# Weight sums of the third branch product issued behind those of the second, and the first gate loads moved behind them

## The reference, cut to what matters

```
o_a = hgrn2_mixer(q_a, f_a, i_a, g_a, lb_table[l], hg_norm[l])
o_b = swa_mixer(q_b, k_b, v_b, positions, sw_sinks[l])
y_a = o_a @ w_proj_a[l]          # (512 x 1024) @ (1024 x 2048)
y_b = o_b @ w_proj_b[l]
merged = sigmoid(gate_a) * y_a + sigmoid(gate_b) * y_b
x = x + merged @ w_out[l]
```

## Time and profile before

| what | value |
|---|---|
| median of 3 runs | 2690.0 us (2689.77 to 2694.65) |
| span of the profiled execution, first to last instruction | 2690.4 us |
| time of the profiled execution beside its span | not recorded apart; the span stands for it |
| PE busy | 2647.6 us (98%) |
| DVE, ACT, POOL busy | 1820.0, 1374.9, 540.6 us |
| moved by DMA | 466.79 MB, 174 GB/s on average |
| longest single wait of PE behind DVE | 7.2 us, in the branch projections |

### The profile page before, as it was taken

How to read it: one execution, slowest core, us unless ns; L and a number is a source line. 1 busy time by engine, 2 the same in 40 slices (tenths; PEclk the granted TensorE clock), 3 DMA queues, 4 the chain that set the end, 5 groups by cost and what they waited for, 6 DMA issues and landing times.

```text
span 2690.4 us, 33239 instructions
## 1 busy us (share of the span) xinstructions
PE 2647.6 (98%) x12726; PEld 2195.0 (82%) x12726; DVE 1820.0 (68%) x2116; ACT 1374.9 (51%) x1692; POOL 540.6 (20%) x390
## 2 busy tenths in 40 slices
PE   8999999999999989999999999999999999999998
PEld 7888888888888778778887888888888888888887
DVE  5865555777666768788458555666655568778787
ACT  6544444645546654545455444444444445544446
POOL 7121112000023222211241122111112212121311
PEclk9999999999999999999999999999999999999999
DMA  8887887532232299875358888787787888798975
GB/s 275 213 196 198 193 184 176 149 89 80 82 92 73 83 256 242 212 200 137 98 157 219 175 170 173 173 198 170 170 179 167 177 213 194 196 208 237 187 213 133
DMA packets 323681, 466.79 MB, mean 174 GB/s; under 512 B 30840, under 2 KB 139728, under 8 KB 320976
## 3 DMA queue, kind: packets, MB, share of 16 engines
q0 software_dynamic: 88672, 170.94, 36.9%
q1 hardware_dynamic: 231936, 288.33, 33.7%
q10 hardware_dynamic: 2928, 5.56, 0.6%
HBM read 430.43 MB, written 34.34 MB: 173 GB/s over the span
## 4 chain that ended last, share of the span: by engine, by line
PE 69%; DVE 4%; DMA 4%; issue 4%; ACT 1%; POOL 1%; DVEq 0%; ACTq 0%; POOLq 0%
PE psum L1186 12%; PE psum L1188 12%; PE psum L1187 12%; PE psum L1607 9%; PE psum L1608 9%; PE psum L1609 9%; DMA f_raw<-in_w_down 1%; PE psum L1369 1%; PE psum L1860 1%; PE psum L1567 1%; PE psum L1568 1%; PE psum L1569 1%; DMA m_tot<-in_w_proj_a 1%; DVE f_lo L3331 1%; DMA out_last<-in_w_out 0%
## 5 line engine op out<-in xcount | busy, mean ns | idle before, releaser
L3552 DVE TENSOR_TENSOR f_lo<-f_raw,f_hi 128x1024 fp32r<-128x1024 f32 x458 | 558.9, 1223 | 398.6 <-ACT f_hi L2572 397.5
L2572 ACT ACTIVATE f_hi<-f_raw 128x1024 fp32r<-128x1024 f32 x460 | 486.6, 1060 | 620.8 <-PE psum L1609 309.8
L1140 POOL DMA_DIRECT2D f_raw<-in_w_up x132 | 158.9, 1204 | 662.3 <-DVE f_lo L3552 619.7
L2893 DVE TENSOR_TENSOR fr_lo<-fr_raw,fr_hi 128x1024 fp32r<-128x1024 f32 x140 | 171.2, 1224 | 158.1 <-ACT fr_hi L2024 157.9
L2024 ACT ACTIVATE fr_hi<-fr_raw 128x1024 fp32r<-128x1024 f32 x140 | 148.4, 1061 | 197.9 <-PE psum L1321 99.7
L1059 POOL TENSOR_TENSOR w_lo<-w_raw,w_hi 128x1024 fp32r<-128x1024 f32 x55 | 136.8, 2502 | 534.6 <-ACT w_hi L1950 526.3
L1186 PE MATMUL psum<-op_hi,w_lo 128*128 128x512 f32 x576 | 233.5, 405 | 0.0
L1188 PE MATMUL psum<-op_hi,w_hi 128*128 128x512 f32 x576 | 224.9, 391 | 0.0
L1187 PE MATMUL psum<-op_lo,w_hi 128*128 128x512 f32 x576 | 224.7, 390 | 0.0
L1159 POOL DMA_DIRECT2D f_raw<-in_w_down x70 | 86.1, 1452 | 285.3 <-DVE f_lo L3552 276.5
L1607 PE MATMUL psum<-f_hi,pa_lo 128*128 128x512 f32 x352 | 137.2, 390 | 0.5 <-DVE f_lo L3552 0.5
(11 more groups left out here) (522 smaller groups left out, 6674.5 us busy)
## 6 DMA issues: line engine op xcount, KB each, us to landing
f_raw<-in_w_up POOLq DMA_DIRECT2D x132, 512.0 KB, 6.6
f_raw<-in_w_gate SPq DMA_DIRECT2D x88, 512.0 KB, 3.8
f_raw<-in_w_down POOLq DMA_DIRECT2D x70, 512.0 KB, 9.1
f_raw<-in_w_down SPq DMA_DIRECT2D x66, 512.0 KB, 5.8
w_raw<-in_w_in SPq DMA_DIRECT2D x64, 512.0 KB, 3.9
fr_raw<-in_w_in SPq DMA_DIRECT2D x60, 512.0 KB, 4.5
fr_raw<-in_w_in POOLq DMA_DIRECT2D x60, 512.0 KB, 7.5
f_raw<-in_w_up SPq DMA_DIRECT2D x44, 512.0 KB, 4.6
```

Source lines behind the costliest of these rows:

```text
L1140: pool.dma_start(raw_pieces(x, slot), up_block(n, p, c), accum_op=ALU.add).then_inc(raw_added[c], 16)
L2572: act.activation(f_split(i)[0][:, :], split_source(i)[:, :], ACT.Copy).then_inc(f_hi_ready, 1)
L2893: dve.tensor_tensor(fr_lo[front_slot(i)][:, :], front_source(i)[:, :], fr_hi[front_slot(i)][:, :].bitcast(F32), ALU.subtract).then_inc(f_l ...
L3552: dve.tensor_tensor(lo[:, :], split_source(i)[:, :], hi[:, :].bitcast(F32), ALU.subtract).then_inc(f_lo_ready, 1)
```

## The change

Three edits, all in the order in which transfers are issued; no computation changes.

```
-        TOTAL_ADDS = [(0, 1), (1, 1), (0, 2), (0, 6), (1, 2), (1, 6), (2, 1), (2, 2), (2, 6), (3, 1), (3, 2), (3, 6)]
+        TOTAL_ADDS = [(0, 1), (0, 2), (1, 1), (0, 6), (1, 2), (1, 6), (2, 1), (2, 2), (2, 6), (3, 1), (3, 2), (3, 6)]
@@ SP
-            for name in gate_order(0):
+            def first_gate(name):
                 sp.dma_start(mixed_rows(0, name), gate_block(0, name)).then_inc(S("gate_b_in0"), 16)
+
+            for x in range(2):
+                sp.wait_ge(f_lo_ready, mixed_at(0, 1) + x + 1)
+                first_gate(gate_order(0)[x])
             sp.wait_ge(S("sw_o_done"), HEADS)
             for c in range(2):
                 mixed_load(0, "22", c)
+            for x in range(2, 4):
+                first_gate(gate_order(0)[x])
@@ POOL
             for n, p in TOTAL_ADDS:
                 add_total(n, p)
-                if (n, p) == (1, 1) or n and p == 2:
-                    add_low(n if p == 2 else 0)
+                if p == 2:
+                    add_low(n)
```

## The result

The changed kernel took 2694.6 us (median of 20 runs), the one before 2690.6 (20 runs). The ratio is 1.0016, with a 95% interval from 1.0010 to 1.0021, so 2.7 to 5.6 us longer: a loss, though a change of 0.16% lies within the 0.2% that the prediction counted as the same. With 20 runs of each kernel the interval is narrower than that. The forecast was 2689.0. The profiled execution took 2694.8 us, its span is 2693.0.

The account below looks back on a forecast made before the run. PE, busy 2647.6 of 2690.4 us, was taken as the bound, with the stage near its DMA limit; removing the wait minus DMA debt nets 1.2 us: 2690.4 - 1.2 = 2689.2 span, 2689 for the runs, range 2685 to 2694.

Parts of the forecast that it names:

- The wait removed: At (0,2) in the branch projections: PE's wait goes, ceiling 10.0 us, of which 7.18 idle and 2.87 lower clock.
- The gates: At (0,3)c1: gate pieces issued later hold DVE's first multiply, a PE wait of 2.5 us, leaving 7.5 of 10.0.
- rows 9: Profile rows of the kernel before: SP's fourth load from 958.73 took 13.2 us, which would give a wait of 0.6.
- the bound of 7.1: At (0,3)c1: PE's wait in us if the last gate piece again takes 19.7 us to land.
- the old wait: PE's wait at (0,2) in the kernel before: 7.18 us idle, with 2.87 us more from the lower clock behind it.
- The DMA debt: Branch projections: 5.1 us of gate transfers move behind 952, against 4.2 us of idle DMA time in the old wait.
- the balance: Gate transfer time less idle DMA time of the old wait: work up to any later point ends 0.9 us later.
- The place that decides: At the sum for (1,2)c1: slack 2.1 us less 0.9 of delay leaves PE a gain of 1.2 us.
- the first rival: POOL's sums keep their turns and SP's loads carry the debt, so 7.5 us are gained: 2682.5; chance 0.28.
- The slower one: Rival: POOL's sums lose their turns, (1,2)c1 lands at 1009.7, time 2695, or 2698 with a clock drop; chance 0.18.
- The signs named as wrong: No PE waits from 966 to 1007, or one over 5 us or lowering the clock, or one later at (2,1).

Follow-up runs that it names:

- low_first: Changed kernel with block 0's two `m_low` transfers issued directly behind the sums (0,1) instead of behind (0,2); 2688.7 us, ratio 0.9993 to the kernel before.
- low_later_gates_late: Kernel before with block 0's `m_low` transfers behind the sum for (0,2) and the change's late gate loads; 2692.2 us, ratio 1.0010.
- gates_only: Kernel before with only the change's gate loads, the sums in the old order; 2688.6 us, ratio 0.9994; run again 2689.8 us, 0.9997.
- split_sem: Changed kernel with a semaphore for each pair of gate pieces, so the first multiply needs only the first pair; 2698.2 us, ratio 1.0028 to before.
- gates_four: Changed kernel with all four gate pieces issued at 953 us, ahead of the `m_b22` loads; 2694.8 us, ratio 1.0013 to the kernel before.
- adds_only: Kernel before with only the new list of sums, the gates early as before; 2689.6 us, ratio 0.9995.
- low_later: Kernel before with block 0's two `m_low` transfers behind the sum for (0,2), gates and sums for (1,1) early; 2689.1 us, ratio 1.0000.

## Why the prediction was wrong

*The wait removed.* Right. The sum for (0,2)c0 was issued at 953.29 (with the stage 1.09 us later, the 951.95 of the prediction) and there is no wait at (0,2).

*The gates.* This is the step that failed, in its size: "I take 2.5 us, at (0,3)c1. Of the 10.0 us, 7.5 are left there." Place and mechanism were right. The last piece took 19.7 us, the upper bound of the earlier trace rows, and not the 13.2 of the earlier trace rows, though it was issued at the place of rows 9. PE waited 5.79 us for it, and the chunk was 1.23 + 5.79 = 7.02 us late, close to the bound of 7.1: the 1.23 us at (0,3)c0, for `m_b22`, only took the first part of the delay. Behind the wait PE lost 2.57 us more to the clock (0.50 from 983.64 to 988.93), which the prediction had counted only for the old wait. Nor did this wait lie inside the later ones ("The gates' wait lies inside this and is not added"): it stood by itself.

*The DMA debt.* The idea was right and its size too small. "5.1 us spent before 952" counted the gates alone. Measured from the start of the stage, 6.4 us of full DMA time are lost in the first 20 us: the sums for (1,1) and the `m_low` transfers had also filled that stretch, and moving them back empties it. After 60 us, near (1,2)c1, 2.7 us are still missing, where the balance was to be 0.9.

*The place that decides.* "The last transfer for which that matters is the sum for (1,2)c1" failed: it released ACT at 1001.61, with 6.5 us to go until PE took the chunk at 1008.12 (before 1002.64 and 1007.08). The sums kept their turns, as the first rival had it: with both queues loaded, POOL's moved 337 packets and SP's 338 from 965 to 970 us, 335 and 334 from 970 to 975, 334 and 342 from 975 to 980 (DMA queues of the kernel after). SP's loads carried the debt, and they were not slack: first the gates, then `m_low` of block 1. The sentence against that rival, "SP's starved loads are the gates, which hold DVE", described the result, but no time was worked out from it.

*The rivals.* The first had its turns right and its time wrong (2682.5). The slower one came nearer to the time (2695 to 2698 against 2694.6), for a wrong reason: no sum for (1,2) was late. Its own sum is off too: 54 us from 954.5 end at 1008.5, not 1009.7, so its times should read 2694 to 2697. The signs named as wrong came true: a wait over 5 us (5.79) with a clock of 0.50 behind it, and one at (2,1), 0.84 us.

*Two smaller slips.* (1,1) starts 6 chunks after the end of (0,5), near 983, and not 8; it had time even so, for PE never waited there. And the span did not stand for the time of the profiled execution, as the section on the result shows.

What stays open: the medians differ by 4.0 us and the two traces show 1.1 in the stage; that the execution traced before was slow for its kernel accounts for some 1.6 of the difference. The runs show that filling the hole takes the loss back (low_first), not how each of the 4 us comes about, and not that a loss needs the hole: low_later_gates_late has a share of 0.87 and an interval just above 1, which overlaps that of the change. Why it is slower than gates_only, whose share is lower, is not settled.

## What to carry to other kernels

Where transfers bound a stage, count what the DMA engines move up to a time, not only how late one transfer lands: a wait that is removed by reordering can come back at the next late transfer, as it did in split_sem (5.07 us at (2,1)), gates_four (8.07 us at (0,3)c0) and adds_only (4.72 us at (2,1)). Two edits that each leave a stretch filled can empty it together (here a DMA share of 0.80 and 0.78 alone, 0.55 together), so look at the issue times of all queues in that stretch, and for a transfer whose inputs are ready earlier. Here moving two such transfers 14 us forward took back the whole loss (low_first, 0.9993), while removing the visible wait took back none (split_sem, 1.0028).

## What the runs showed of the hardware

Waits of nearly one length can have different prices at the clock. Behind the 5.79 us in the kernel after, the chunk took 5.29 us, 2.57 more than the 2.72 at a granted clock of 1.00; the clock read 0.50 from its first matmul to its last. Behind 5.67 us in low_later_gates_late it took 4.21 us, 1.49 more; the clock read 0.50 from 982.94 to 985.70 and 0.94 from there to its end at 987.15 (timeline of PE, low_later_gates_late):

```profile
982.94 0.79 PE L1573 MATMUL psum<-m_hi,ms_lo 128*128 128x512 f32 x1 [5.67 <-DVE m_lo L3197]
...
987.15 0.39 PE L1573 MATMUL psum<-m_hi,ms_lo 128*128 128x512 f32 x1
```

A short wait can have a price too, and the clock need not fall at once. In low_first, after the 2.17 us at 978.54, the stretch right behind it ran at a granted clock of 0.60 (stretches of low_first):

```profile
978.00:981.00 3.00, 2.46 (x6) 1.98 (x7) 3.00 (x4) 1.06 (x1) 1.20 (x1) 0.60 1.11 247
```

In low_later, after 2.37 us at 973.55, the chunk began at a clock of 1.00 (its first matmul took 0.50 us, not 0.78) and the clock fell about 1.2 us later (974.5 to 975.0 reads 0.80, 975.0 to 975.5 reads 0.50):

```profile
973.00:976.00 3.00, 2.45 (x8) 2.01 (x9) 3.00 (x4) 2.04 (x3) 1.20 (x1) 0.80 1.10 262
976.00:979.00 3.00, 3.00 (x10) 2.30 (x10) 3.00 (x3) 0.54 (x1) 0.00 (x0) 0.63 1.13 219
```

The price was the same: the 24 matmuls behind the wait took 7.16 us in low_first and 7.20 in low_later, 1.7 to 1.8 more than two chunks of 2.72. Behind the 1.16 us of adds_only the clock did not fall (it read 1.00 from 974 to 984, and the chunk took 2.81 us). The 0.80 and 0.63 of low_later are means over stretches that held two levels: in steps of 0.2 to 0.3 us the clock from 972 to 982 read 1.00, then 0.50 from 975.0 to 978.2, then 1.00 again, and something else only in the two steps in which it changed (0.51 and 0.97). So in these two runs waits of 2.17 and 2.37 us were followed by a clock of 0.50, in one at once and in the other when matmuls had begun again. That is one reason to judge a kernel by the sum of its waits and not by the longest: split_sem's longest, 5.07 us, is shorter than the 5.79 of the change, its four waits come to 10.0 against 8.1, and its ratio is the highest of all.
